# Attention steps in another order, projections over three pairs of PSUM banks, and scores issued two units ahead between transposes

## The chip, the cores and the metric

The kernel runs on one core of one Trainium2 chip. The metric is the device time of one execution, in microseconds (us); less is better. The core's engines are named as in the profile: PE is TensorE's matmul row and PEld its weight loads, DVE is VectorE, ACT is ScalarE, POOL is GpSimd and SP is SyncE, which here only issues DMAs.

## What is computed

Two layers of a streaming encoder, over 1024 prompt tokens and 64 sample tokens, width 1024. Each layer is

```python
xn = rmsnorm(x, norm_pre)
a_x, a_g, b_q, ..., c_v, c_g = split(xn @ w_in)
y_a = rg_lru(causal_conv(a_x)) * silu(a_g)            # width 512
y_b = top-k sparse attention, 4 heads * silu(b_g)     # width 256
y_c = differential attention, 4 heads * silu(c_g)     # width 256: softmax1 - lam * softmax2, normed per head
x = x + rmsnorm(concat(y_a, y_b, y_c) @ w_out, norm_post)
```

The attention is causal by chunks of 64 tokens, so query tile t (128 tokens) reads 128 (t + 1) keys; the sample tile reads 1024 cached keys and its own 64. All is computed in fp32. The kernel returns x of the last layer and each layer's states.

## The kernel before

Each layer has a front (input projection, convolution and recurrence, the indexer's scores, the search for the top-k threshold) and then the attention stage, which alone the change touches. The attention stage takes the nine query tiles in the order 7, sample, 6, 0, 1, 2, 3, 4, 5 (`ORDER`). Each tile has four C units (one head each, with two softmax maps, except in the sample tile, where a C unit has one map of stacked queries) and four B units (two in the sample tile), 70 units in all. `schedule()` (L123) writes out one list, `STEPS`, and every engine walks through the same list and takes what is its own, in order:

- `qk` i, m: TensorE computes the scores of a map into one of two PSUM slots (L1692 to L1702), VectorE takes the negative maximum (L1454), ScalarE the exponential and its row sum (L1141).
- combining unit i (`combine`, L575): VectorE takes the reciprocal of the sum and, for a C unit, mixes the two maps with `scalar_tensor_tensor` (L585 to L597). The transposes of the unit wait for it (L1714). In the kernel before it is tied to the first `qk` of the next unit (L1449).
- `tr` i, g: TensorE transposes up to four blocks of 128 keys into one PSUM bank (L1717); ScalarE (C units) or VectorE (B units) copies them out (L570). All groups and all `ytr` share this one bank, so each waits for the copy of the one before (L1712).
- `pv` i: TensorE multiplies the transposed weights with the values into the output bank (L1736); VectorE scales the result (`divide`, L599: L613 to L627, where a C unit also sums its squares). In the kernel before it is tied to the first `tr` of the next unit (L1463).
- `ytr` n: the finished heads of the n-th tile, once GpSimd has gated them, are transposed (L1746) and copied out by ScalarE (L1157).
- `proj` n, q: 16 steps of the output projection of tile n (8 for the sample tile), L1775 and L1770, into PSUM banks 2 and 3 (`mixb`, L394). Step 0 waits until the rows of the tile before have been taken out of them (`mix_drained`, L1755). `QUOTA` (L90) says how many steps a unit may carry.
- `square` n on ScalarE (L1178, L1172, L1175), 1/sqrt on GpSimd (L937, L939), `rows` n on VectorE (L1481, L1477), the residual added on GpSimd (L946), the store on SP (L735).

A tile is called wide here where it has more than 512 keys (7, sample, 6, 4, 5: two or three groups of transposes) and narrow otherwise (0 to 3: one group). Scores use PSUM banks 0 to 2 and 3 to 5; outside the sample tile the second slot is banks 4 and 5, so that 2 and 3 are free for the projections. In a wide unit i the list is: first map of `qk` i+1, `rows`, second map, `proj`, `tr` i 0, `proj`, `pv` i-1, the other groups of `tr` i, and `ytr` in the third unit of a tile. In a narrow one: first map, one `proj`, `pv` i-1, `rows`, second map, the other `proj` steps, `tr` i. When a projection ends, the next one may start two units later (`hold`, L144). GpSimd prepares the padded queries of the tiles to come at certain `qk` steps (L902 to L908).

## Time and profile before

| | us |
|---|---|
| median of three runs | 1717.11 (1715.88 to 1722.72) |
| the profiled execution | 1713.17 |
| its span, first to last instruction | 1711.4 |
| TensorE busy | 1579.6 (92% of the span) |
| VectorE busy | 1130.6 (66%) |
| ScalarE busy | 626.8 (37%) |
| GpSimd busy | 425.3 (25%) |
| granted TensorE clock, mean | 0.973 |

The first layer's attention stage lies at 463 to 860 us of the span, the second one's at about 1311 to 1711. Rows of a timeline give the start, the duration, the engine, the line, the operation with its tiles, and in brackets the idle time before it with what ended it. A duration of a matmul includes its way through the array, so neighbouring rows overlap; a step's length is best read from start to start.

### The profile page before, as it was taken

The page shows a single profiled execution, that of the slowest core. Times are in us where ns is not written, and L with a number is a line of the kernel's source. Part 1 is how long each engine was busy: PE and PEld are TensorE (multiplying, and loading weights), DVE is VectorE, ACT ScalarE, POOL GpSimd, SP SyncE. Part 2 cuts the span into 40 slices and gives each one's busy share as a digit, 9 for nine tenths or more (in the row PEclk, how much of TensorE's full clock was granted, in tenths as well). Part 3 has the DMA queues.
Part 4 walks back from the last instruction along what each step waited for, and adds up shares of the span by engine and source line. Part 5 has one row for each costly group of instructions (what it writes and reads, how often), then busy time and mean ns, then how long its engine had stood idle before and what let it go on. Part 6 is the DMA issues. An engine that isn't in the chain of part 4 may idle for free. (4 is left out here: it accounts for less than half of the span.)

```text
span 1711.4 us, 21022 instructions
## 1 busy us (share of the span) xinstructions
PE 1579.6 (92%) x7276; PEld 1083.2 (63%) x7298; DVE 1130.6 (66%) x2456; ACT 626.8 (37%) x1227; POOL 425.3 (25%) x540
## 2 busy tenths in 40 slices
PE   6999999999988889999859999999999888899996
PEld 3566566688876755567435665666888667555663
DVE  3478999948963655465134789999589646545550
ACT  2285520228143333333022756202280433333330
POOL 2001621520020344342120016205200213444411
PEclk9999999999998999999979999999999999999999
DMA  5100001321050311110151000013210503111101
GB/s 175 53 25 25 25 25 50 100 76 35 1 185 4 113 38 58 40 38 32 49 187 53 25 25 25 25 50 99 65 47 0 183 6 117 42 52 37 51 24 56
DMA packets 39177, 99.19 MB, mean 58 GB/s; under 512 B 8672, under 2 KB 27616, under 8 KB 34720
## 3 DMA queue, kind: packets, MB, share of 16 engines
q1 hardware_dynamic: 39072, 97.85, 17.3%
q8 instruction: 59, 0.97, 0.2%
q14 instruction: 46, 0.38, 0.1%
HBM read 66.84 MB, written 18.14 MB: 50 GB/s over the span
## 5 line engine op out<-in xcount | busy, mean ns | idle before, releaser
L1551 PE MATMUL ps<-r_xn,r_w 128*128 128x384 f32 (+1 forms) x1728 | 555.3, 473 | 12.3 <-DVE r_xn L1218 7.5
L1551 PEld LDWEIGHTS ps<-r_xn,r_w 128*128 128x128 f32 x1728 | 326.0, 191 | 195.7 <-issue 18.5
L1319 DVE TENSOR_SCALAR_CACHE_REDUCE r_ix<-r_sc,smi 128x768 bf16<-128x768 f32 (+6 forms) x380 | 342.0, 962 | 2.2
L1141 ACT ACTIVATE r_sc<-ps,sm 128x1024 f32<-128x1024 f32 (+8 forms) x204 | 155.7, 764 | 346.4 <-DVE sm L1454 339.2
L1454 DVE TENSOR_REDUCE sm<-ps 128x1 f32<-128x1024 f32 (+8 forms) x204 | 157.2, 784 | 121.8 <-PE ps L1699 52.1
L1627 PE MATMUL ps<-r_w,r_xn 128*128 128x256 f32 x1024 | 223.4, 380 | 0.0
L1627 PEld LDWEIGHTS ps<-r_w,r_xn 128*128 128x128 f32 x1024 | 193.9, 190 | 27.3 <-issue 1.0
L1736 PEld LDWEIGHTS ps<-r_vg,r_w 128*128 128x128 f32 (+1 forms) x1176 | 149.9, 194 | 52.9 <-issue 25.4
L1736 PE MATMUL ps<-r_vg,r_w 128*128 128x64 f32 (+1 forms) x1176 | 151.9, 274 | 6.3 <-DVE r_w L613 3.0
L1717 PE MATMUL ps<-ident,r_sc 128*128 128x128 f32 (+1 forms) x684 | 118.0, 282 | 39.1 <-ACT r_w L570 28.1
L1775 PE MATMUL ps<-r_xn,r_ag 128*128 128x512 f32 x256 | 137.5, 644 | 14.4 <-DVE r_res L1481 11.4
L1717 PEld LDWEIGHTS ps<-ident,r_sc 128*128 128x128 f32 (+1 forms) x684 | 83.7, 148 | 95.4 <-issue 46.8
L1775 PE MATMUL ps<-r_xn,r_vg 128*128 128x512 f32 x256 | 126.8, 604 | 0.1
L1281 DVE SCALAR_TENSOR_TENSOR r_sc<-r_vg,sm,r_sc 128x384 f32<-128x384 f32 (+6 forms) x98 | 97.8, 998 | 28.9 <-ACT r_vg L1056 23.4
L1056 ACT ACTIVATE r_vg<-ps 128x384 f32<-128x384 f32 (+6 forms) x112 | 88.4, 795 | 29.9 <-PE ps L1588 24.3
L570 DVE COPY r_w<-ps 128x512 f32<-128x512 f32 (+3 forms) x104 | 58.7, 565 | 60.3 <-PE ps L1717 59.3
L613 DVE TENSOR_SCALAR r_w<-ps,sm 128x64 f32<-128x64 f32 x128 | 35.7, 279 | 80.0 <-PE ps L1736 80.0
L1696 PE MATMUL ps<-kst_c,qc_hi 128*128 128x512 f32 (+3 forms) x192 | 79.4, 414 | 3.5 <-ACT r_sc L1141 2.0
L570 ACT COPY r_w<-ps 128x512 f32<-128x512 f32 (+3 forms) x112 | 55.0, 491 | 61.9 <-PE ps L1717 61.9
L1775 PEld LDWEIGHTS ps<-r_xn,r_ag 128*128 128x128 f32 x256 | 46.9, 208 | 41.4 <-issue 25.8
L783 POOL COPY sm<-r_ax 128x3 f32<-128x3 f32 x8 | 4.0, 501 | 271.3 <-ACT r_ax L995 271.3
L1588 PE MATMUL ps<-iks,iqs 128*128 128x384 f32 (+3 forms) x160 | 68.7, 500 | 1.5 <-ACT iqs L1038 1.5
(244 smaller groups left out, 2068.5 us busy)
## 6 DMA issues: line engine op xcount, KB each, us to landing
r_w<-w_in SPq DMA_DIRECT2D x28, 1024.0 KB, 4.9
r_xn<-w_out SPq DMA_DIRECT2D x2, 4096.0 KB, 13.5
y<-r_res SPq DMA_DIRECT2D x16, 512.0 KB, 2.9
r_vg<-x SPq DMA_DIRECT2D x8, 512.0 KB, 9.9
r_xn<-ckT SPq DMA_DIRECT2D x2, 2048.0 KB, 8.3
r_xn<-vcache SPq DMA_DIRECT2D x2, 2048.0 KB, 13.8
o_v<-r_vg SPq DMA_DIRECT2D x4, 1024.0 KB, 11.1
r_sc<-x SPq DMA_DIRECT2D x8, 512.0 KB, 4.9
```

The costliest lines, as they stand in the source:

```text
L570: ins = copy(pT[i % 2][:, k0:k1, 0:r], src[:, 0:k1 - k0, 0:r])
L1056: drains_x(nc.scalar.activation(dst, src, ACT.Relu, scale=scale), key)
L1141: ins = nc.scalar.activation(ex[2 * (i % 2) + m][0:r, 0:w], on_slot(s, w, r), ACT.Exp, bias=negm[0:r, c:c + 1], accum_out=den[0:r, c:c + 1])
L1281: ins = vec.scalar_tensor_tensor(sc[t][0:r, 0:w], src, iw[0:r, t, h:h + 1], sc[t][0:r, 0:w], ALU.mult, ALU.add)
L1319: ins = vec.tensor_scalar(unsel[t][0:rows(t), :], sc[t][0:rows(t), :], b, None, op, ALU.add, accum_out=cnt[0:rows(t), c:c + 1])
L1454: vec.tensor_reduce(negm[0:r, c:c + 1], on_slot(s, w, r), X, ALU.max, negate=True)\
L1551: ins = nc.tensor.matmul(on_ring(key, cn), w[:, k, P * s:P * (s + 1)], xnT[:, k, c0:c0 + cn], start=(k == 0), stop=(k == KT - 1))
L1627: ins = nc.tensor.matmul(on_ring(key)[:, BW * (t - t0):BW * (t - t0 + 1)], xnT[:, k, P * t:P * (t + 1)], w[:, k, :], start=(k == 0), stop= ...
L1696: ins = nc.tensor.matmul(out, q, kst[kind][:, h, c0:c0 + cn], start=(n2 == 0), stop=(n2 == 1 and not more))
L1717: ins = nc.tensor.transpose(tbank[0:kn, P * (k - 4 * g):P * (k - 4 * g) + r], ex[2 * (i % 2)][0:r, P * k:P * k + kn], ident[0:r, 0:r])
L1736: ins = nc.tensor.matmul(obank[0:r, 0:vals.shape[1]], pT[i % 2][0:kn, k, 0:r], vals, start=(k == 0), stop=(k == nk - 1))
L1775: ins = nc.tensor.matmul(mixb[:, half, :], yk, wo[:, k, BANK * half:BANK * (half + 1)], start=(k == 0), stop=(k == KT - 1))
```

## The change

Three PSUM places for the projections instead of one, `combine` and `divide` as steps of their own, another order of the list, and the scores of unit i+2 between the transposes of unit i in the sample tile and in the B units of wide tiles.

- `mix_place`: projections of the 2nd and 4th tile in the order go to banks 4 and 5, that of the 8th to banks 0 and 1, the others to banks 2 and 3. For this the second slot of narrow tiles moves to bank 1 (`on_slot`). A projection waits only for the rows of the tile that had the same place before. The scores of the first unit of tile 4 get a wait for the fourth tile's rows and for the map before.
- `qk` is split: `exp` is ScalarE's part and may stand later in the list than `qk`. `comb` and `div` are VectorE's and stand in the list.
- `ytr` moves from behind the transposes of its unit to ahead of them. `rows` comes one unit (wide) or two units (narrow) after its projection's end, in wide tiles ahead of `comb`. Where the place differs, the next projection follows without a pause. The projection of the 8th tile is kept until after the last unit.
- In the sample tile and the B units of wide tiles the order of unit i is: `rows`, `ytr`, one `proj`, `tr` i 0, `qk` i+2 (if units i+1 and i+2 have one map each), `proj`, `tr` i 1, `pv` i-1, `div` i-1, `tr` i 2, `exp` i+2, and then the next unit begins with `comb` i+1. This is so in 14 of the 70 units.

```diff
@@ -89,6 +89,8 @@
 YTR = 2
+NARROW_MIX = (1, 3)
+NARROW_END = 7
 LAST_ROWS = [("tm", "cv", 3), ("tm", "cv", 4)]
+def mix_place(n):
+
+    return 1 if n in NARROW_MIX else 2 if n == NT - 2 else 0
+def same_place(n):
+
+    return [m for m in range(n) if mix_place(m) == mix_place(n)]
@@ -127,49 +139,76 @@
+    def scores(i):
+
+        new = []
+        if begun[0] <= i < len(units):
+            begun[0] = i + 1
+            if i:
+                new.append(("comb", i - 1))
+            for m in range(maps_of(i)):
+                new += [("qk", i, m), ("exp", i, m)]
+        return new
     def take(i, most):
         new = []
         while waiting and most and i >= hold[0]:
-            n, q = waiting.pop(0)
+            n, q = waiting[0]
+            if n >= NT - 2 and i < len(units):
+                break
+            waiting.pop(0)
             new.append(("proj", n, q))
             most -= 1
             if q == proj_steps(ORDER[n]) - 1:
                 new.append(("square", n))
-                finish.append(n)
-                hold[0] = i + 2
+                late = 1 if width(units[min(i, len(units) - 1)][0]) > BANK else 2
+                finish.append((i + late, n))
+                if mix_place(n + 1) == mix_place(n):
+                    hold[0] = i + late + 1
         return new
...
-        pv = [("pv", i - 1)] if i else []
-        steps += nxt[:1]
+        pv = [("pv", i - 1), ("div", i - 1)] if i else []
+        n = NTH[i]
+        ytr = []
+        if i - FIRST[n] == YTR and n:
+            ytr = [("ytr", n - 1)]
+        nxt = scores(i + 1)
+        if not nxt:
+            nxt = [("comb", i)]
         if len(groups) == 1:
-            steps += take(i, 1) + pv + rows_now + nxt[1:] + take(i, quota - 1) + groups
+            steps += nxt[:3] + take(i, 1) + pv + rows_now + nxt[3:] + ytr + take(i, quota - 1) + groups
+        elif t == SAMPLE or (True and kind == "B"):
+
+            steps += nxt
+            steps += rows_now + ytr + take(i, 1) + groups[:1]
+            ahead = []
+            if i + 2 < len(units) and maps_of(i + 1) == maps_of(i + 2) == 1:
+                ahead = [("qk", i + 2, 0), ("exp", i + 2, 0)]
+                begun[0] = i + 3
+            steps += ahead[:1] + take(i, quota - 1) + (groups[1:2] + pv if ahead else pv + groups[1:2])
+            steps += groups[2:] + ahead[1:]
         else:
-            steps += rows_now + nxt[1:] + take(i, 1) + groups[:1] + take(i, quota - 1) + pv + groups[1:]
+            steps += rows_now + nxt + ytr + take(i, 1) + groups[:1] + take(i, quota - 1) + pv + groups[1:]
...
-        steps += new + ([("rows", new[-1][1])] if new[-1][0] == "square" else [])
-    steps.append(("ytr", NT - 1))
+        steps += new + ([("rows", new[-1][1])] if new[-1][0] == "square" and new[-1][1] < NT - 2 else [])
+    steps += [("ytr", NT - 1), ("rows", NT - 2)]
@@ -391,7 +430,8 @@
-        mixb = ps[:, 2 * BANK:4 * BANK].rearrange("p (s b) -> p s b", s=2)
+        banks = ps[:, :].rearrange("p (s b) -> p s b", b=BANK)
+        mixbs = [banks[:, 2:4, :], banks[:, 4:6, :], banks[:, 0:2, :]]
@@ -494,7 +534,7 @@
-                slot = slot[:, BANK:]
+                slot = slot[:, BANK:] if width(ATT[key[1]][0]) > BANK else ps[0:r, BANK:2 * BANK]
@@ -1446,8 +1487,6 @@
-                            if m == 0 and i >= 1:
-                                combine(dve, link, i - 1, first[i - 1])
@@ -1455,18 +1494,16 @@
-                            i, g = s[1], s[2]
-                            if g == 0 and i == len(ATT) - 1:
-                                combine(dve, link, i, first[i])
-                            if ATT[i][1] == "B":
-                                evac_pT(dve, vec.tensor_copy, i, g)
-                            if g == 0 and i >= 1:
-                                divide(dve, i - 1, link)
-                        elif s[0] == "pv" and s[1] == len(ATT) - 1:
+                            if ATT[s[1]][1] == "B":
+                                evac_pT(dve, vec.tensor_copy, s[1], s[2])
+                        elif s[0] == "comb":
+                            combine(dve, link, s[1], first[s[1]])
+                        elif s[0] == "div":
                             divide(dve, s[1], link)
@@ -1669,6 +1706,9 @@
+                            if h == 0 and m == 0 and n == NARROW_END:
+                                pe.wait_ge(mix_drained, NARROW_MIX[-1] + 1)
+                                wait_drained(pe, MAPS[SLOT[s] - 1])
@@ -1750,13 +1790,17 @@
-                                if n:
-                                    pe.wait_ge(mix_drained, n)
-                                else:
-                                    last = FIRST[ORDER.index(SAMPLE) + 1] - 1
-                                    wait_drained(pe, ("qk", last, 0))
-                                    wait_drained(pe, ("qk", last - 1, 0))
+                                if same_place(n):
+                                    pe.wait_ge(mix_drained, same_place(n)[-1] + 1)
+                                if mix_place(n) == 2:
+                                    wait_drained(pe, MAPS[-1])
+                                    wait_drained(pe, MAPS[-2])
+                                if not same_place(n):
+                                    wide = FIRST[ORDER.index(SAMPLE) + (1 if n == 0 else 2)] - 1
+                                    wait_drained(pe, ("qk", wide, 0))
+                                    wait_drained(pe, ("qk", wide - 1, 0))
```

## Rows read from the trace of the kernel before

**Rows 1.** Windows, PE alone: stretch, length, busy (instructions), granted clock, DMA share, GB/s
```profile
499.40:516.50 17.10, 17.10 (x120) 1.00 0.10 30
516.50:555.90 39.40, 32.44 (x179) 0.87 0.00 1
555.90:599.10 43.20, 38.61 (x244) 0.92 0.31 112
599.10:742.00 142.90, 131.44 (x613) 0.95 0.17 50
742.00:773.70 31.70, 29.57 (x172) 1.00 0.04 11
773.70:821.00 47.30, 44.58 (x270) 1.00 0.15 49
821.00:857.00 36.00, 29.62 (x67) 0.90 0.09 31
```
**Rows 2.** Waits of PE, 462 to 860 us: total, times, longest
```profile
PE ps L1775 <- DVE r_res L1481: 5.7, 3, 3.1
...
PE ps L1770 <- DVE r_res L1481: 1.4, 1, 1.4
```
**Rows 3.** Timeline, end of the first layer: start, us, engine, line, operation
```profile
829.71 3.60 PE L1775 MATMUL ps<-r_xn,r_vg 128*128 128x512 f32 x8
...
833.34 1.02 ACT L1178 ACTIVATE r_w<-ps 128x1024 bf16<-128x1024 f32 x1 [19.27 <-PE ps L1775]
...
834.35 0.59 ACT L1157 ACTIVATE r_vg<-ps 128x512 f32<-128x512 f32 x1
...
835.47 1.28 DVE L1481 SCALAR_TENSOR_TENSOR r_res<-ps,sm,r_ix 128x1024 f32<-128x1024 f32 x1 [13.91 <-POOL sm L939]
836.81 6.58 PE L1775 MATMUL ps<-r_xn,r_ag 128*128 128x512 f32 x8 [3.07 <-DVE r_res L1481]
```
**Rows 4.** Timeline of PE, B units of tile 7
```profile
505.64 0.61 PE L1717 MATMUL ps<-ident,r_sc 128*128 128x128 f32 x4
...
507.92 1.90 PE L1736 MATMUL ps<-r_vg,r_w 128*128 128x64 f32 x16
509.65 0.61 PE L1717 MATMUL ps<-ident,r_sc 128*128 128x128 f32 x4
```
**Rows 5.** Timeline of DVE: divide and reciprocal of B units
```profile
625.55 0.28 DVE L613 TENSOR_SCALAR r_w<-ps,sm 128x64 f32<-128x64 f32 x1
625.86 0.16 DVE L585 RECIPROCAL sm<-sm 128x1 f32<-128x1 f32 x1
```
**Rows 6.** Timeline, a C unit of the sample tile
```profile
533.97 0.29 DVE L616 TENSOR_SCALAR r_w<-ps,sm 64x64 f32<-64x64 f32 x1 [1.25 <-PE ps L1736]
...
535.17 0.16 DVE L590 TENSOR_TENSOR sm<-sm 64x1 f32<-64x1 f32 x1
...
535.88 0.42 PE L1717 MATMUL ps<-ident,r_sc 128*64 128x128 f32 x1 [0.68 <-ACT r_w L570]
```
**Rows 7.** Timeline, a C unit of tile 4 (640 keys, wide)
```profile
747.32 1.08 PE L1775 MATMUL ps<-r_xn,r_ag 128*128 128x512 f32 x2
...
749.40 0.58 ACT L570 COPY r_w<-ps 128x512 f32<-128x512 f32 x1
```
**Rows 8.** Timeline, C units of tile 3 (512 keys, narrow)
```profile
707.26 0.68 ACT L1141 ACTIVATE r_sc<-ps,sm 128x512 f32<-128x512 f32 x1
...
708.07 0.60 PE L1717 MATMUL ps<-ident,r_sc 128*128 128x128 f32 x4
708.16 0.16 DVE L592 RECIPROCAL sm<-sm 128x1 f32<-128x1 f32 x1 [0.78 <-ACT r_sc L1141]
...
709.39 0.68 DVE L1454 TENSOR_REDUCE sm<-ps 128x1 f32<-128x512 f32 x1
...
713.17 0.60 PE L1717 MATMUL ps<-ident,r_sc 128*128 128x128 f32 x4
```
**Rows 9.** Timeline of PE, end of the second layer
```profile
1687.26 3.70 PE L1775 MATMUL ps<-r_xn,r_ag 128*128 128x512 f32 x8 [3.07 <-DVE r_res L1481]
```

More of the change, by code:

```diff
@@ L129, in schedule @@
     hold = [FIRST[ORDER.index(SAMPLE) + 1] + FIRST_PROJ]
-    def qk(i):
-        return [("qk", i, m) for m in range(maps_of(i))]
+    begun = [0]
+    def scores(i):
[7 more added lines that the diff above has]
+        return new
     def take(i, most):
@@ L142, in take @@
                 new.append(("square", n))
-                finish.append(n)
-                hold[0] = i + 2
+                late = 1 if width(units[min(i, len(units) - 1)][0]) > BANK else 2
+                finish.append((i + late, n))
+                if mix_place(n + 1) == mix_place(n):
+                    hold[0] = i + late + 1
         return new
-    steps += qk(0) + LAST_ROWS
+    steps += scores(0) + LAST_ROWS
     for i, (t, kind, h) in enumerate(units):
@@ L150, in schedule @@
         groups = [("tr", i, g) for g in range(-(-nk // 4))]
-        nxt = qk(i + 1) if i + 1 < len(units) else []
-        rows_now = [("rows", finish.pop(0))] if finish else []
+        rows_now = [("rows", finish.pop(0)[1])] if finish and finish[0][0] <= i else []
         quota = QUOTA.get(t, 0)
-        pv = [("pv", i - 1)] if i else []
-        steps += nxt[:1]
-        if len(groups) == 1:
-            steps += take(i, 1) + pv + rows_now + nxt[1:] + take(i, quota - 1) + groups
-        else:
-            steps += rows_now + nxt[1:] + take(i, 1) + groups[:1] + take(i, quota - 1) + pv + groups[1:]
-        n = NTH[i]
-        if i - FIRST[n] == YTR and n:
-            steps.append(("ytr", n - 1))
+        pv = [("pv", i - 1), ("div", i - 1)] if i else []
[6 more added lines that the diff above has]
+            nxt = [("comb", i)]
+        if len(groups) == 1:
+            steps += nxt[:3] + take(i, 1) + pv + rows_now + nxt[3:] + ytr + take(i, quota - 1) + groups
[8 more added lines that the diff above has]
+            steps += groups[2:] + ahead[1:]
+        else:
+            steps += rows_now + nxt + ytr + take(i, 1) + groups[:1] + take(i, quota - 1) + pv + groups[1:]
+        if ytr:
             waiting += [(n - 1, q) for q in range(proj_steps(ORDER[n - 1]))]
@@ L165, in schedule @@
     hold[0] = last
-    steps.append(("pv", last - 1))
-    steps += [("rows", n) for n in finish]
+    steps += [("pv", last - 1), ("div", last - 1)]
+    steps += [("rows", n) for _, n in finish]
     while waiting:
@@ L1132, in _ @@
                     for s in STEPS:
-                        if s[0] == "qk":
+                        if s[0] == "exp":
                             i, m = s[1], s[2]
@@ L1140, in _ @@
                                 act.wait_ge(t_filled, last + 1)
-                            ins = nc.scalar.activation(ex[2 * (i % 2) + m][0:r, 0:w], on_slot(s, w, r), ACT.Exp,
+                            ins = nc.scalar.activation(ex[2 * (i % 2) + m][0:r, 0:w], on_slot(("qk", i, m), w, r), ACT.Exp,
                                                        bias=negm[0:r, c:c + 1], accum_out=den[0:r, c:c + 1])
-                            drains(ins, s)
+                            drains(ins, ("qk", i, m))
                             nmap += 1
@@ L1162, in _ @@
                             act.wait_ge(mix_filled, n + 1)
+                            mixb = mixbs[mix_place(n)]
                             if n >= 1:
@@ L1469, in _ @@
                             r = rows(ORDER[n])
+                            mixb = mixbs[mix_place(n)]
                             dve.wait_ge(rso_ready, n + 1)
```

1 line of the change is left out of this document (added).

## The prediction

> **What bounds the kernel now.** I first read the stages of the first layer's attention as a table of TensorE's busy time [rows 1]. TensorE is the bound: from 499 to 857 us it works in most of every stage, and what is lost is idle time between its own instructions (0 of 17.1 us in the four B units of tile 7, 7.0 of 39.4 in the sample tile, 11.5 of 142.9 in the narrow tiles, 2.1 and 2.7 in the two wide tiles behind them) and a clock under 1.00. The second layer runs the same list of steps and loses the same waits. TensorE's work isn't changed by the edit, so the question is only how much idle time the new list leaves. The waits of TensorE say who ends them [rows 2]: 5.7 and 1.4 us a layer go to projections that wait until the rows of the tile before have left the two PSUM banks that all tiles share; 3.07 of them lie at the end of the layer [rows 3], 4.0 inside. That is what the alternating banks remove. Of the rest most is a transpose waiting for the copy of the group before it.
>
> I then wrote out the step list of both kernels and laid the durations of the trace along every place where the lists differ. An estimate below means such a chain.
>
> **Two units ahead in the B units of tile 7.** Now a B unit takes 4.01 us and TensorE is full: its second group of transposes starts at 505.64 and that of the next unit at 509.65 [rows 4]. Nothing is left to hide there. The new list puts the scores of unit i+2 between the two groups, but puts `div` of unit i-1 ahead of `comb` of unit i+1 on VectorE, and TensorE's next step behind `pv` i-1 is the transpose that needs this `comb`. So each such unit gets a round trip: values end, VectorE divides (0.31 us to the reciprocal's start) and takes the reciprocal (0.16) [rows 5], and the signal back costs 0.06 (VectorE's row of 835.47 ends at 836.75, the matmul that waits for it starts at 836.81 [rows 3]; I take 0.1). With the 0.17 us by which the next transposes now overlap the values' row (507.92 + 1.90 against 509.65 [rows 4]) I take 0.8 us for each; 1.0 where the divided unit is a C unit (it also squares) or the next one is the sample tile's (a longer `comb`). Four of them lie in a row here: 3.6 us. Bounds: 0.5 to 1.2 each.
>
> **The sample tile.** Now a C unit waits for the first copy and 0.68 us for the second [rows 6], which with the overlap that is lost makes 1.2 to 1.9 a unit. The new list hides both behind scores and values, but sets the round trip in their place, and it is long: from the divide's start at 533.97 to the end of `comb` at 535.33 are 1.36 us [rows 6]. Against some 6.4 us of such waits in the stage (7.0 idle in all [rows 1]) I get 6.8 with the moved `ytr`: +0.4. The same list for tile 6 and the first B units of tile 4 has a projection step (0.86 us: four of them run from 829.71 to 833.14 [rows 3]) between `pv` and the transpose, which covers the trip: 0.
>
> **`ytr` moved ahead of the transposes.** It shares their bank, so tr i.0 now waits for ScalarE's copy of `ytr` (0.59 us [rows 3]), which stands behind the exponential of the second map. In a wide C unit scores end at 747.3, where the projection starts, and ScalarE's next copy starts at 749.40 [rows 7]; so a transpose behind it could start at 747.3 + 2.1 + 0.6 + 0.1 = 750.1, and TensorE has only the four transposes of `ytr`, some 0.45 us, for these 2.8. The old place of `ytr` waits too, for one copy alone. For tile 6, wider still and with no projection in between: +1.5, between 0 and 3.
>
> **Narrow tiles.** The mix waits of these tiles go (4.0 us), and the projection steps that were held back for them run earlier. The price is that they run out. A projection of tile n can't begin before `ytr` n, and the list has 80 steps for 96 places, so the gaps gather in front of `ytr` 4 and 5, in C units 38, 39 and 46, 47; now they lie mostly in B units, which are cheap. What an uncovered C unit costs: at 708 the unit takes 5.1 us from transpose to transpose (708.07 to 713.17 [rows 8]), of which three projection steps of 0.86 are 2.6, so TensorE has 2.5 us of its own. The loop through the others is: exponential of the second map to the start of `comb` 0.90, `comb` 1.23 up to the next max, two max of 0.68 [rows 8], a divide with its square of about 0.5 (estimated from the 0.31 of the divide above) between them and a signal: 4.1 us. So 1.6 us idle a unit, 1.3 more where `rows` (1.28 us on VectorE [rows 3]) falls in it, and then `ytr` with no projection step behind it, about 3.5. Laid out with the durations of each width this is 6.1 us ahead of `ytr` 4, 7.0 ahead of `ytr` 5 and 1 elsewhere: 14 against 11.5. +2.5. Bounds: if half of it hides, -4; if VectorE also loses time to GpSimd, +5.
>
> **Tiles 4 and 5 (the wide ones at the end).** Nine projection steps that covered them are used up in the narrow tiles, two more are kept for the end. In units 54 to 56 nothing stands between tr.0, `pv` and tr.1: scores end at 747.3, tr.1 can't start before 749.40 + 0.58 + 0.1 = 750.1, and TensorE has the values (ten matmuls, of which 16 take 1.73 us [rows 4]: 1.1) and 0.4 of transposes for these 2.8, so 1.3 idle each. Besides, `rows` stands now ahead of `comb` in VectorE's order, one unit after the projection ends. From the end of a projection, about 833.1: the square starts at 833.34, `rows` on VectorE at 835.47 and ends at 836.75 [rows 3], so 3.6 us; then `comb` 1.5 at these widths, and the next transposes wait for it: 1.4 us at unit 55, 2.8 at unit 65. By chain: tile 4 7.5 us idle against 2.1 (+5.4), tile 5 9.1 against 2.7 (+6.4; in it two bare round trips of 1.0 and 0.8, and `ytr` 7 with one projection step behind it, 2.0). Bounds of the two together: +5 (a half) to +14.
>
> **End of the layer.** Projection 8 no longer waits for `rows` 7: now 3.07 us idle [rows 3]. It still needs `ytr` 8, whose copy (834.35) ends at 834.94, so it starts at 835.1 instead of 836.8: -1.7. In the first layer the clock fell in this gap (eight matmuls took 6.58 us [rows 3], in the second layer 3.70 [rows 9]); if the shorter gap prevents that, -3 once.
>
> **The other moved steps.** GpSimd pads queries at the first scores of a tile; of the scores moved ahead none passes a gating step of GpSimd. SP's stores and loads of `rows` go one or two units later, and POOL's add of `rows`; the next tile's `rows` is at least two units on. The waits on `same_place` come after rows that are long done. The new wait of the first scores of unit 54 has nothing late before it. Cost 0, and 1 us for each if that cover were gone.
>
> **Sum.** 3.6 + 0.4 + 1.5 + 2.5 + 5.4 + 6.4 - 1.7 = 18.1 us a layer, 36 in two, less 3 for the clock: +33. The profiled execution took 1713.2 us (span 1711.4); that makes 1746. It lies 3.9 under the median of the three runs, 1717.1, so I forecast 1750.
>
> **Rivals.** (a) Faster: the uncovered places cost no more than they do in the B units now, since VectorE and ScalarE then have no rows to do in between. Then all the idle time of the narrow tiles that such waits make, 8 of the 11.5 us, and 1.7 at the end are won, 3.6 + 0.4 go to the round trips, and a clock fall of 3 us a layer goes with the gaps: about -8.5 a layer, 1700. For it: the waits it removes are measured ones [rows 2]. Against it: [rows 7, 8], which show the chains longer than the work left beside them. It decides if `comb` doesn't stand in the way, and the loop of 4.1 us says it does. The Trainium skill (Perfetto Trace Analysis, Matmuls) says that independent matmul groups should rotate through different PSUM banks so that the evacuation of one overlaps the next; by that rule alone the change wins, as in (a). (b) No change: the terms are half of what I take and more clock is won than lost, 1717. (c) Slower still: the new gaps of 2 to 3.6 us, four or five a layer against two or three now, each bring the clock to its lower level of 1.2 GHz, as the gap before 836.81 did [rows 3]. The stage from 821 to 857 had 0.90 granted [rows 1], 3.6 us lost. Three more such falls a layer: +20 us, 1770. Against it: in the second layer the same gap of 3.07 us brought no fall [rows 9]. The Trainium skill (TensorE: Matmul & The Clock Gate, Why this matters for your kernels) asks for no long idle gaps between bursts of matmuls; by that rule this rival is the likeliest. That the change doesn't do what it says is excluded: the list has the early scores in 14 of 70 units.
>
> **Chances.** Forecast, slower by 10 to 45 us: 0.60. (c): 0.14. (b): 0.12. (a): 0.14. A measurement of this kernel can tell some 0.5% (8.6 us) from no change. Faster 0.14, same 0.12, slower 0.74. The forecast's own range is 1730 to 1762; the range given, 1712 to 1768, takes in (b) and half of (c), and leaves out (a) and the worst of (c), some 0.2.
>
> **What would show it.** Right: in the profile after, TensorE's transposes wait for VectorE's `comb` (now L585, L590, L597); tile 7's B units take 4.8 us; gaps of over 2 us at the transposes of units 40, 48, 56, 64, 65; waits on `rows` gone; TensorE idle near 57 us a layer against 40. Wrong: the B units still at 4.0, or wide tiles at the end no longer than now by more than the moved projections account for. The forecast fails if VectorE runs `div` late without TensorE waiting, or if the copies are ready sooner in shorter units than the chains say.

## The result, and the profile after

| | before | after |
|---|---|---|
| median of four runs each | 1716.5 us | 1758.8 us (1756.9 to 1760.8) |
| ratio | | 1.025 (95% interval 1.022 to 1.029) |
| span of the profiled execution | 1711.4 us | 1755.1 us |
| granted TensorE clock, mean | 0.973 | 0.956 |

The changed kernel is slower by 42 us. In the changed kernel the transposes are L1757 (they were L1717), the values L1776 (L1736), the scores L1736 to L1742 (L1696 to L1702), the projections L1819 (L1775), `comb` L625 to L637 (L585 to L597), `div` L653 (L613), the copies of transposes L610 (L570), the copy of `ytr` L1197 (L1157), `rows` L1518 (L1481).

The pages' groups of instructions, the two that matter (busy time and mean ns | idle time before them and what ended most of it), before and then after:

```profile
L1717 PE MATMUL ps<-ident,r_sc 128*128 128x128 f32 (+1 forms) x684 | 118.0, 282 | 39.1 <-ACT r_w L570 28.1
...
L1775 PE MATMUL ps<-r_xn,r_ag 128*128 128x512 f32 x256 | 137.5, 644 | 14.4 <-DVE r_res L1481 11.4
```
```profile
L1757 PE MATMUL ps<-ident,r_sc 128*128 128x128 f32 (+1 forms) x684 | 122.7, 290 | 80.2 <-ACT r_vg L1197 24.5
...
L1819 PE MATMUL ps<-r_xn,r_ag 128*128 128x512 f32 x256 | 133.5, 631 | 3.3 <-ACT r_vg L1197 2.7
```

The projections hardly wait any more: 3.3 us over both layers instead of 14.4. The transposes wait 80 us instead of 39. TensorE's waits in the first layer, the answer to [rows 2] (engine, line, what ended the wait: total us, times, longest):

```profile
PE ps L1757 <- ACT r_vg L1197: 12.8, 6, 3.0
PE ps L1757 <- ACT r_w L610: 9.8, 8, 2.7
PE ps L1757 <- DVE r_sc L637: 6.0, 3, 3.9
PE ps L1757 <- DVE sm L625: 5.5, 7, 1.1
```

None is on `rows` any more, where [rows 2] had 5.7 and 1.4 (and a line that it doesn't show, for the rows of the sample tile, 1.3). In their place stand the copy of the moved `ytr`, the operation of `comb` that mixes two maps (L637) and the reciprocal of the B units (L625).

To lay the two kernels side by side I cut both layers at the first matmul of the values of units 0, 7, 13, 21, 53, 61 and 69, because the list has these once a unit in the same order. The windows of the first layer of the changed kernel (stretch, length, busy time and instructions of TensorE, granted clock, share of DMA, GB/s):

```profile
484.20:523.50 39.30, 33.87 (x225) 1.00 0.45 162
523.50:565.60 42.10, 34.97 (x205) 0.88 0.03 7
565.60:607.50 41.90, 37.64 (x237) 0.92 0.30 114
607.50:751.40 143.90, 131.34 (x601) 0.96 0.16 48
751.40:799.20 47.80, 42.09 (x210) 0.79 0.11 34
799.20:840.00 40.80, 31.18 (x193) 0.92 0.08 27
```

And of the kernel before, the last three:

```profile
604.10:744.20 140.10, 128.47 (x585) 0.95 0.17 50
744.20:782.60 38.40, 36.44 (x213) 1.00 0.14 42
782.60:819.70 37.10, 34.38 (x210) 1.00 0.06 17
```

With the same windows in the second layer, "idle" being length less busy time, and the projection steps that the list has in each stage:

| stage (values of units) | length before, layers 1 / 2 | after | idle before | after | projection steps before, after |
|---|---|---|---|---|---|
| tile 7 and sample (0 to 13) | 79.3 / 78.2 | 81.4 / 79.8 | 10.8 / 10.9 | 12.5 / 13.8 | 0, 0 |
| tile 6 (13 to 21) | 40.6 / 38.5 | 41.9 / 40.4 | 3.0 / 3.8 | 4.3 / 4.3 | 6, 6 |
| narrow tiles (21 to 53) | 140.1 / 136.7 | 143.9 / 142.5 | 11.6 / 11.5 | 12.6 / 8.9 | 74, 82 |
| tile 4 (53 to 61) | 38.4 / 38.4 | 47.8 / 48.0 | 2.0 / 2.0 | 5.7 / 6.7 | 14, 12 |
| tile 5 (61 to 69) | 37.1 / 37.0 | 40.8 / 40.7 | 2.7 / 2.7 | 9.6 / 9.6 | 12, 4 |
| sum | 335.5 / 328.8 | 355.8 / 351.4 | 30.2 / 30.9 | 44.7 / 43.3 | 106, 104 |

A step takes 0.86 us of TensorE, so lengths of a stage compare only with its steps beside them: tile 5 grew by 3.7 us although eight steps, 6.9 us of work, had left it.

The attention grew by 20.3 and 22.6 us. The stretch between the two layers' windows (521.6 us before, 522.2 after) and the end behind the second one (41.3 and 41.5) stayed, with the two moved steps (1.7 us) now in each of them. 27 us of the 43 are idle time (14.5 + 12.4). The rest is matmuls that take longer: busy time went from 305.3 to 311.1 and from 297.9 to 308.1 us, with two projection steps fewer inside (1.7 us a layer), so 19 us for the same work. The granted clock shows why. The 10 us windows around units 54 to 56, and the two waits that lie in them:

```profile
740.00:750.00 10.00, 10.00 (x55) 1.00 0.11 27
750.00:760.00 10.00, 5.76 (x28) 0.71 0.03 8
760.00:770.00 10.00, 8.53 (x38) 0.50 0.31 106
770.00:780.00 10.00, 10.00 (x46) 0.77 0.08 20
780.00:790.00 10.00, 10.00 (x58) 1.00 0.05 12
```
```profile
754.74 0.48 PE L1757 MATMUL ps<-ident,r_sc 128*128 128x128 f32 x1 [2.35 <-ACT r_w L610]
...
759.83 1.09 PE L1757 MATMUL ps<-ident,r_sc 128*128 128x128 f32 x4 [1.89 <-DVE r_sc L637]
```

TensorE stands still for 2.35 us before 754.74 and 1.89 us before 759.83, and then runs ten microseconds at 0.50, the lower level of 1.2 GHz: four transposes take 1.09 us there, and 0.63 us at 1.00. Before the change this tile had 1.00 throughout [rows 1].

### The profile page after: what moved, and what is told of

Same layout as the page of the kernel before. It is cut to its first block and busy times, and to the rows that moved or that the text cites. A ratio compares the mean times of both kernels' runs of the same rounds, so it can differ in the third digit from the quotient of the medians.

```text
span 1755.1 us, 21012 instructions
## 1 busy us (share of the span) xinstructions
PE 1599.2 (91%) x7276; PEld 1102.4 (63%) x7298; DVE 1136.3 (65%) x2456; ACT 626.1 (36%) x1227; POOL 422.8 (24%) x540
## 5 line engine op out<-in xcount | busy, mean ns | idle before, releaser
L1588 PE MATMUL ps<-r_xn,r_w 128*128 128x384 f32 (+1 forms) x1728 | 559.0, 475 | 12.5 <-issue 7.9
L1757 PE MATMUL ps<-ident,r_sc 128*128 128x128 f32 (+1 forms) x684 | 122.7, 290 | 80.2 <-ACT r_vg L1197 24.5
L1776 PEld LDWEIGHTS ps<-r_vg,r_w 128*128 128x128 f32 (+1 forms) x1176 | 158.3, 204 | 50.1 <-issue 22.3
L1757 PEld LDWEIGHTS ps<-ident,r_sc 128*128 128x128 f32 (+1 forms) x684 | 84.3, 150 | 139.3 <-issue 64.1
L1776 PE MATMUL ps<-r_vg,r_w 128*128 128x64 f32 (+1 forms) x1176 | 160.4, 284 | 8.4 <-ACT r_w L610 7.2
L1819 PE MATMUL ps<-r_xn,r_ag 128*128 128x512 f32 x256 | 133.5, 631 | 3.3 <-ACT r_vg L1197 2.7
L1819 PE MATMUL ps<-r_xn,r_vg 128*128 128x512 f32 x256 | 128.5, 612 | 0.0
L653 DVE TENSOR_SCALAR r_w<-ps,sm 128x64 f32<-128x64 f32 x128 | 36.1, 282 | 134.8 <-PE ps L1776 134.8
L610 DVE COPY r_w<-ps 128x512 f32<-128x512 f32 (+3 forms) x104 | 58.9, 566 | 70.9 <-PE ps L1757 70.1
L610 ACT COPY r_w<-ps 128x512 f32<-128x512 f32 (+3 forms) x112 | 55.2, 492 | 86.1 <-PE ps L1757 86.1
L1736 PE MATMUL ps<-kst_c,qc_hi 128*128 128x512 f32 (+3 forms) x192 | 81.6, 425 | 4.6 <-ACT r_sc L1181 3.0
L1736 PE MATMUL ps<-kst_c,qc_lo 128*128 128x512 f32 (+3 forms) x192 | 69.9, 376 | 0.0
```

Source lines behind the costliest of these rows:

```text
L610: ins = copy(pT[i % 2][:, k0:k1, 0:r], src[:, 0:k1 - k0, 0:r])
L1588: ins = nc.tensor.matmul(on_ring(key, cn), w[:, k, P * s:P * (s + 1)], xnT[:, k, c0:c0 + cn], start=(k == 0), stop=(k == KT - 1))
L1736: ins = nc.tensor.matmul(out, q, kst[kind][:, h, c0:c0 + cn], start=(n2 == 0), stop=(n2 == 1 and not more))
L1757: ins = nc.tensor.transpose(tbank[0:kn, P * (k - 4 * g):P * (k - 4 * g) + r], ex[2 * (i % 2)][0:r, P * k:P * k + kn], ident[0:r, 0:r])
L1776: ins = nc.tensor.matmul(obank[0:r, 0:vals.shape[1]], pT[i % 2][0:kn, k, 0:r], vals, start=(k == 0), stop=(k == nk - 1))
L1819: ins = nc.tensor.matmul(mixb[:, half, :], yk, wo[:, k, BANK * half:BANK * (half + 1)], start=(k == 0), stop=(k == KT - 1))
```

## The experiments

Each starts from the changed kernel, unless it says otherwise. "Attention" is the time from the values of unit 0 to those of unit 69 in the two layers; the changed kernel has 355.8 and 351.4, the kernel before 335.5 and 328.8.

| kernel | median us | against after | attention, us | projection steps inside |
|---|---|---|---|---|
| before | 1714.8 to 1716.5 | | 335.5 / 328.8 | 106 |
| after | 1758.8 | | 355.8 / 351.4 | 104 |
| e1 no early scores in B units | 1752.6 | -6.2 | 352.6 / 349.8 | 104 |
| e2 `comb` before `div` | 1738.4 | -20.4 | 346.2 / 343.6 | 104 |
| e3 `ytr` back | 1745.3 | -13.5 | 349.3 / 346.5 | 104 |
| e4 `rows` behind `comb` | 1742.5 | -16.3 | 349.0 / 347.4 | 104 |
| e6b even pace | 1721.8 | -37.0 | 337.5 / 331.5 | 102 |
| h1 no addition on GpSimd | 1744.0 | -14.8 | 353.1 / 351.1 | 104 |
| o1 old order, two PSUM places | 1735.6 | -23.2 | 346.0 / 347.0 | 112 |
| o2 o1 with the end mended | 1725.8 | -33.0 | 346.4 / 346.1 | 112 |
| o3 o2 with even pace | 1697.2 | -61.6 | 325.3 / 325.6 | 104 |
| g1 all four amended | 1680.2 | -78.6 | 316.6 / 316.1 | 102 |
| g2 g1 without early scores | 1692.7 | -66.1 | 322.6 / 322.8 | 102 |
| g3 g1, early in the sample tile only | 1682.2 | -76.6 | 316.8 / 315.9 | 102 |

The kernel before was timed beside each group of these; its medians were 1714.8 to 1716.5 us, single executions 1706.4 to 1727.0. The part ahead of the attention is the same code in all of them, and its length still differs: the values of unit 0 begin between 482.8 and 487.4 us. So a difference of two or three microseconds between two kernels isn't read below. Where the steps inside differ, 0.86 us for each belongs to them: o1 has six more than the kernel before, 5.2 us a layer.

**The round trip behind the early scores.**

```diff
-        elif t == SAMPLE or (True and kind == "B"):
+        elif t == SAMPLE or (False and kind == "B"):
```

> The changed kernel, but the B units of wide tiles issue no scores two units ahead (the sample tile still does). Theory of the round trip (divide, then `comb`, then the signal back, 0.7 to 0.9 us a unit where no projection step lies between): the four B units of tile 7 go back from 21.0 to about 17.1 us and units 66 and 67 lose their waits of 0.8 and 0.7, so -5.5 us a layer, -11 in all, about 1748. Rival, that the early scores cost nothing and the time went to the clock alone: tile 7 stays at 21 us and the whole is within 3 us of 1759. Rival, that the early scores also hide something now (the copies in the wide B units): tile 7 falls to 18 or 19 only, -4 to -6 in all.

TensorE's waits in tile 7's B units went, and those of 0.81 and 0.67 us behind units 66 and 67 too. A B unit of tile 7 is back at 4.0 us (505.10 to 509.12), so the third explanation, that the early scores hide something there, is out. But a new wait of 0.82 us, for a copy on ScalarE, stands in the first unit of the sample tile. Idle time fell by 3.5 and 1.9 us in the two layers, the median by 6.2: right direction, about half of the -11 expected. In the first layer the sample tile then ran at 0.84 instead of 0.88, which took part of it back. (The ratio to the kernel before, 1.020, is known to 0.006, some 10 us, so the size stays rough.) The next kernel keeps the early scores and changes only VectorE's order (`rden` holds the reciprocals, now in four places by i % 4):

```diff
                 begun[0] = i + 3
+                combed.add(i + 1)
+                pv = pv[:1] + [("comb", i + 1)] + pv[1:]
...
-        rden = sm[:, 160:164]
+        rden = sm[:, 228:236]
...
```

> The changed kernel, with `comb` of unit i+1 ahead of `div` of unit i-1 on VectorE in the 14 units with early scores, and the reciprocals in four places instead of two so that neither overwrites the other. Theory of the round trip: what TensorE waits for is only the order on VectorE, so the waits on `comb` in tile 7 (0.67 to 0.86) and in the sample tile (0.98 to 1.30) go: -3 in tile 7, -3 to -4 in the sample tile, -1 in tile 5, so -7 to -8 us a layer, about 1744. Rival, that the exponential is what is late (it stands behind the last group's copy on ScalarE): then `comb` can't run earlier, and less than 5 us of the whole go. Rival, that the early scores themselves cost: 0.

-20.4 us, somewhat more than expected. The timeline of the changed kernel and then of this one, the same B unit of tile 7 (start, us, engine, line, operation, in brackets the idle time before and what ended it):

```profile
509.15 0.29 DVE L653 TENSOR_SCALAR r_w<-ps,sm 128x64 f32<-128x64 f32 x1 [0.35 <-PE ps L1776]
...
509.47 0.16 DVE L625 RECIPROCAL sm<-sm 128x1 f32<-128x1 f32 x1
509.78 0.63 PE L1757 MATMUL ps<-ident,r_sc 128*128 128x128 f32 x4 [0.67 <-DVE sm L625]
```
```profile
505.19 0.15 DVE L628 RECIPROCAL sm<-sm 128x1 f32<-128x1 f32 x1
505.72 0.61 PE L1760 MATMUL ps<-ident,r_sc 128*128 128x128 f32 x4
505.92 0.28 DVE L656 TENSOR_SCALAR r_w<-ps,sm 128x64 f32<-128x64 f32 x1 [0.57 <-PE ps L1779]
```

In the first the reciprocal stands behind the divide, and the transposes start 0.31 us after the reciprocal's start. In the second it is done 0.4 us before the transposes, which wait for nothing. Units 0 to 13 took 72.2 and 72.0 us (after: 81.4 and 79.8; before: 79.3 and 78.2). So with `comb` ahead of `div` these units are 7.1 and 6.2 us shorter than before the change; 2.8 and 3.1 of that are idle time, the rest is the clock of the sample tile (0.89 and 0.92 before, 1.00 here). Of the 9.2 and 7.8 us that this one swap won against the changed kernel, 4.5 and 6.0 are idle time; the clock of the sample tile went from 0.88 and 0.96 to 1.00.

**`ytr` behind the transposes again.**

```diff
-            steps += nxt[:3] + take(i, 1) + pv + rows_now + nxt[3:] + ytr + take(i, quota - 1) + groups
+            steps += nxt[:3] + take(i, 1) + pv + rows_now + nxt[3:] + take(i, quota - 1) + groups
...
-            steps += rows_now + nxt + ytr + take(i, 1) + groups[:1] + take(i, quota - 1) + pv + groups[1:]
+            steps += rows_now + nxt + take(i, 1) + groups[:1] + take(i, quota - 1) + pv + groups[1:]
+        steps += ytr
```

> The changed kernel with `ytr` again behind the transposes of its unit. Theory that the moved `ytr` costs what its copy stands behind on ScalarE (waits of 2.25, 2.91, 2.96, 1.47 and 2.28 us a layer behind that copy, against some 0.5 us each in the old place): -7 to -9 us a layer, -14 to -18 in all, about 1743, and a lower-clock stretch or two less. Rival, that these units are short of covering work whatever the place of `ytr` (no projection step left in them): the waits only change their name to the copies of the transposes, and less than 5 us of the whole go.

-13.5 us: just short of the theory's lower edge. But it holds only in the wide tiles (tile 6 -3.6 and -2.1 us, tile 4 -3.5 and -3.6, tile 5 -1.9 and -1.8), and there only in part by the waits: idle time of the whole attention fell by 1.2 us in the first layer and 5.1 in the second, of 6.5 and 4.9 us of length. In the first layer tile 4 even had 0.6 us more idle time and was shorter because its clock was 0.92 instead of 0.79. In the narrow tiles the length stayed (144.4 and 143.6 against 143.9 and 142.5), and the rival is right there. The wait of unit 40, in the changed kernel (with the `rows` ahead of it on VectorE) and in this one:

```profile
680.44 1.28 DVE L1518 SCALAR_TENSOR_TENSOR r_res<-ps,sm,r_ix 128x1024 f32<-128x1024 f32 x1
...
683.43 0.90 PE L1757 MATMUL ps<-ident,r_sc 128*128 128x128 f32 x3 [2.91 <-ACT r_vg L1197]
```
```profile
681.32 0.90 PE L1787 MATMUL ps<-ident,r_w 128*128 128x128 f32 x3 [2.90 <-ACT r_w L611]
```

The same 2.9 us, once in the transposes behind the copy of `ytr`, once in `ytr` behind the copy of the transposes. Both copies stand behind the exponential of the second map on ScalarE, and TensorE has no projection step. In the changed kernel that exponential starts at 682.22, after the maximum that VectorE takes at 681.63, directly behind `rows`: as the prediction had it, `rows` (1.28 us) is in this chain. No run moves `rows` alone in the narrow tiles.

**`rows` behind `comb`.**

```diff
-            steps += rows_now + nxt + ytr + take(i, 1) + groups[:1] + take(i, quota - 1) + pv + groups[1:]
+            steps += nxt[:3] + rows_now + nxt[3:] + ytr + take(i, 1) + groups[:1] + take(i, quota - 1) + pv + groups[1:]
```

> The changed kernel with `rows` behind `comb` and the first maximum of its unit in the C units of wide tiles. Theory that `rows` holds up `comb` in units 55 and 65 (waits of 1.89 and 3.87 us): both go but for some 0.6 us that the missing projection steps leave, so -4 to -5 us a layer, -9 in all, about 1750. Rival, that the units are only short of projection steps: the wait moves to the exponential or to the second maximum that `rows` now delays, and the whole stays within 3 us of 1759.

-16.3 us, where -9 was expected. The wait of 1.89 us ahead of unit 55 went and that of 3.87 us ahead of unit 65 became 1.05. Idle time in tiles 4 and 5 fell by 6.1 us in the two layers, but their length by 14.1: tile 4 ran at 0.85 and 0.92 instead of 0.79 and 0.82, tile 5 at 0.95 instead of 0.92. A microsecond of idle time there went with more than two of length. The attention makes up 10.8 of the 16.3 us; the rest lies in parts whose code is the same.

Unit 65 in the changed kernel shows a second thing:

```profile
816.83 1.28 DVE L1518 SCALAR_TENSOR_TENSOR r_res<-ps,sm,r_ix 128x1024 f32<-128x1024 f32 x1
...
818.19 2.34 POOL L986 TENSOR_TENSOR r_res<-r_res,r_sc 128x1024 f32<-128x1024 f32 x1 [1.73 <-DVE r_res L1518]
...
818.59 2.76 DVE L637 SCALAR_TENSOR_TENSOR r_sc<-r_sc,sm 128x768 f32<-128x768 f32 x1
...
821.49 0.63 PE L1757 MATMUL ps<-ident,r_sc 128*128 128x128 f32 x4 [3.87 <-DVE r_sc L637]
```

`comb` takes 2.76 us while GpSimd adds the residual; where nothing runs beside it, this operation takes 1.02. At unit 55 it is 2.63 against 0.89. So `rows` ahead of `comb` costs twice: its own 1.28 us, and 1.7 us because its addition is released just as `comb` starts. This kernel leaves out nearly all of the residual addition, so its outputs are not the layer's:

```diff
-                            nc.gpsimd.tensor_tensor(res[0:r, :], res[0:r, :], xres[0:r, :], ALU.add)\
+                            nc.gpsimd.tensor_tensor(res[0:r, 0:8], res[0:r, 0:8], xres[0:r, 0:8], ALU.add)\
```

> The changed kernel with GpSimd's addition of the residual (it follows each `rows`) cut to 8 of the 1024 columns, so it leaves out nearly all of that sum; all waits and the order of the list stay. In the changed kernel `comb`'s last operation took 2.63 and 2.76 us at units 55 and 65 while that addition ran (2.34 us), and 1.02 us at 768 columns where none ran. Theory that VectorE's operation with two SBUF inputs stands still while GpSimd adds: both fall to 0.9 and 1.0 us, the waits ahead of units 55 and 65 from 1.89 and 3.87 us to about 0.2 and 2.1, so some 3.4 us a layer and with the clock they bring down 10 to 14 us in all, about 1747. Rival, that these two operations are long for another reason (the order behind `rows`, a slow reading of PSUM before): they stay over 2 us, and the whole within 3 us of 1759.

Unit 65 with it:

```profile
813.53 1.28 DVE L1518 SCALAR_TENSOR_TENSOR r_res<-ps,sm,r_ix 128x1024 f32<-128x1024 f32 x1
...
814.89 0.20 POOL L986 TENSOR_TENSOR r_res<-r_res,r_sc 128x8 f32<-128x8 f32 x1 [2.25 <-DVE r_res L1518]
...
815.28 1.02 DVE L637 SCALAR_TENSOR_TENSOR r_sc<-r_sc,sm 128x768 f32<-128x768 f32 x1
```

The operation is back at 1.02 us (0.88 at unit 55) and the wait ahead of unit 65 at 1.03 us: the stall is GpSimd's. The time also fell by about what was expected, 14.8 us, and yet not for the reason given. The attention became only 2.7 and 0.3 us shorter. Tile 5 lost 3.0 us of idle time and 0.6 us of length, because its clock fell from 0.92 to 0.83; ahead of unit 55 1.55 of the 1.89 us of waiting stayed. Most of the gain lies outside: 6.1 us between the two attentions and 2.3 behind the second one, where the last addition of a layer (2.3 us) stands on the path to its end. In 220 us of the stretch between them, from 40 us behind the attention on, the granted clock was 0.97 and 0.94 in the changed kernel; why, these runs don't show.

**The PSUM places alone, and the pace of the projections.** These three keep the order of the kernel before (`comb`, `div` and `exp` are steps of their own, at their old places). Against that kernel, and beside the banks and waits of the change:

```diff
+def mix_place(n):
+    return 1 if n in NARROW_MIX else 0
...
-                hold[0] = i + 2
+                if mix_place(n + 1) == mix_place(n):
+                    hold[0] = i + 2
```

> The order of the list as before the change (`comb`, `div`, `ytr`, `rows` in their old places, no early scores), with only the second PSUM place for the projections of the 2nd and the 4th tile and no pause where the place differs; the last two tiles share one place as before. Theory that the projection steps run out: the 4.0 us a layer of waits on `rows` inside go, but units 38, 39, 46, 47 and 54 to 55 have no projection step, 1.3 to 1.6 us idle each, so 0 to +4 us a layer, 1716 to 1724. Rival, the bank rule alone: -4 us a layer and some clock, about 1706.

1735.6 us, 1.012 of the kernel before (1.008 to 1.015): +20 us from an edit that removes waits and lets the next projection follow at once. Both expectations were too good. Idle time rose by 4.3 and 3.7 us in the two layers, as the theory had it at its worst; another 10 us are longer matmuls for the same work, which neither counted. The waits on `rows` inside went, and the projection steps ran out. Unit 40's neighbourhood in this kernel:

```profile
675.51 0.88 PE L1769 MATMUL ps<-r_vg,r_w 128*128 128x64 f32 x6 [0.82 <-ACT r_w L603]
...
678.92 0.88 PE L1769 MATMUL ps<-r_vg,r_w 128*128 128x64 f32 x6 [1.29 <-ACT r_w L603]
...
681.30 0.88 PE L1750 MATMUL ps<-ident,r_sc 128*128 128x128 f32 x3 [1.02 <-DVE r_sc L630]
683.31 0.90 PE L1779 MATMUL ps<-ident,r_w 128*128 128x128 f32 x3 [1.14 <-ACT r_w L603]
```

There is no projection between them, and each of these waits for VectorE or ScalarE. Idle time in the narrow tiles is 13.8 and 12.8 us (11.6 and 11.5 before) at a clock of 0.93 and 0.94, against 0.95 and 0.98.

The second kernel gives the last tile's projection banks 0 and 1 and puts `ytr` 8 among the last steps of projection 7:

```diff
-    return 1 if n in NARROW_MIX else 0
+    return 1 if n in NARROW_MIX else 2 if n == NT - 1 else 0
...
+        if n_end(new):
+            new = new[:-5] + [("ytr", NT - 1)] + new[-5:]
...
```

> The kernel of the run before (old order, two places) with the projection of the last tile in banks 0 and 1 and `ytr` 8 between the last steps of projection 7, so that projection 8 waits for nothing. The gap of 3.07 us ahead of projection 8 goes in both layers and the slow stretch behind it in the first one, against the run before: -6 to -9. Rival, that the time comes back as a clock fall elsewhere: -3 or less.

-9.8 us, slightly more than expected. The gap of 3.06 us ahead of projection 8 is gone; from 834.62 on TensorE has no idle time up to the layer's last step. The third changes one number for three of the four narrow tiles:

```diff
-QUOTA = {0: 3, 1: 3, 2: 3, 3: 3, 4: 2, 5: 2, 6: 1}
+QUOTA = {0: 3, 1: 2, 2: 2, 3: 2, 4: 2, 5: 2, 6: 1}
```

> The kernel of the run before with two projection steps a unit instead of three in tiles 1 to 3, so that every unit up to the last has one. Theory that a projection step is worth what it covers: idle time of TensorE in the narrow tiles and tile 4 falls by 6 to 8 us a layer against the run before, and the whole lies under the kernel before the change: 1695 to 1703. Rival, that the copies and `comb` are waited for at any pace: within 4 us of the run before.

-28.5 us against o2, and 0.989 of the kernel before (0.986 to 0.993). Tiles 4 and 5, first in o1, then here:

```profile
753.00:795.20 42.20, 38.95 (x212) 0.88 0.13 38
795.20:832.60 37.40, 34.59 (x211) 1.00 0.09 29
```
```profile
736.80:775.40 38.60, 36.34 (x215) 1.00 0.11 31
775.40:812.70 37.30, 35.87 (x215) 1.00 0.03 13
```

Two more projection steps in each, and tile 4 is still 3.6 us shorter. The same three numbers in the changed kernel; since projection 6 then ends after the last unit, where that list had no `rows` for it, this kernel has a `rows` behind each projection that ends there:

> The changed kernel with the even pace of projection steps (two a unit in tiles 1 to 3) and nothing else; projection 6 now ends behind the last unit, and `rows` 6 follows it. Theory that most of the loss in the narrow tiles and in tiles 4 and 5 is missing cover (the same pace took 28 us from the old order): the waits of 2.9 at units 40 and 48, of 2.35 and 1.89 at 54 and 55, of 2.3 and 3.9 at 64 and 65 shrink to 1 or less each, 9 to 11 us of idle time and two clock falls less a layer, 1725 to 1735. Rival, that the moved `ytr` and `rows` cost the same at any pace: not under 1750.

-37.0 us, more than expected: most of the loss of the change goes with these three numbers. In the attention 10.2 and 10.3 us of it are idle time, 6.4 and 7.9 shorter matmuls for the same work, 1.7 two steps that lie behind it. The narrow tiles took 123.6 and 122.0 us (143.9 and 142.5 after, with 14 steps more, 12 us), all at clock 1.00.

**All of it together.** g1 has e2, e3, e4, e6b and the end of o2; g2 and g3 take the early scores out again, in all 14 units and in the B units.

> The changed kernel with all four amended: `comb` before `div` in the units with early scores, `ytr` behind the transposes, `rows` behind `comb`, the even pace, and `ytr` 8 among the last steps of projection 7. Theory that every loss found is a place in the list and none lies in the early scores or the third PSUM place themselves: the waits that are left are those of the C units of tiles 7 and 6 and of the sample tile's second copy, and the early scores save 3 us a layer in the sample tile, so it lies some 10 us under the old order at even pace (1697): 1682 to 1692. Rival, that the early scores cost what they save once `comb` is right: 1693 to 1700. Rival, that TensorE in the full B units only moves the wait to the copies: over 1700.

> The kernel of the run before without any early scores (14 units back to the plain order of wide units). By the theory the B units stay full either way (4.0 us each), and only the sample tile's waits of 0.68 and 0.61 to 0.97 a unit come back: 5 to 8 us slower than with them, 1688 to 1698. By the rival the two are within 3 us of each other. Against the old order at even pace (1697) it lacks the 1.7 us ahead of projection 7 in each layer: 3 to 5 us less.

> The kernel with all four amended, with early scores in the sample tile alone (not in the B units of tiles 7, 6, 4 and 5). If the B units have nothing to hide, it equals the one with all within 3 us. If a full B unit with early scores still has a wait, it is 2 to 5 us faster than that one; if they hide copies in tiles 4 and 5, as much slower.

g1 is at 1680.2 us, 0.981 of the kernel before (0.978 to 0.984). Its windows, at the same cuts as above:

```profile
484.30:520.30 36.00, 33.39 (x225) 1.00 0.49 175
520.30:557.80 37.50, 32.39 (x207) 0.95 0.03 8
557.80:597.40 39.60, 36.13 (x240) 0.96 0.32 120
597.40:721.70 124.30, 116.18 (x574) 1.00 0.17 51
721.70:759.60 37.90, 36.48 (x216) 1.00 0.10 30
759.60:800.90 41.30, 37.55 (x216) 0.96 0.08 26
```

The narrow tiles and tile 4 run at 1.00, and most of what is left of idle time in tile 5 is 2.64 us at unit 62, the one unit of that tile between two projections that share a place. The four single edits took 9.6, 6.5, 6.8 and 18.3 us from the first layer's attention and 7.8, 4.9, 4.0 and 19.9 from the second one's, 41.2 and 36.6 in sum; together they took 39.2 and 35.3, so inside the attention they hardly overlap. The medians add up less well: 87.2 us for the four and 9.8 for the end as o2 has it, against 78.6 together. Without the early scores it is 12.5 us slower, more than the 5 to 8 expected; units 0 to 13 are 5.1 and 5.9 us longer. Having them in the B units too makes no difference that can be told (2.0 us).

## Why the prediction was right, and where it was not

The forecast was 1750, slower, with 1730 to 1762 of its own; it came to 1758.8. The direction and the named mechanisms stand. The sum came near for a partly wrong reason: inside the attention it had 13 us too much idle time in the two layers and left out 19 us of longer matmuls. That the two nearly cancel is luck. Per layer:

| step, idle time in us | predicted | measured, layers 1 / 2 |
|---|---|---|
| tile 7 and sample (3.6 + 0.4) | +4.0 | +1.7 / +2.9 |
| tile 6, `ytr` | +1.5 | +1.3 / +0.5 |
| narrow tiles | +2.5 | +1.0 / -2.6 |
| tile 4 | +5.4 | +3.7 / +4.7 |
| tile 5 | +6.4 | +6.9 / +6.9 |
| sum of idle time inside | +19.8 | +14.5 / +12.4 |
| longer matmuls for the same work | 0 | +7.5 / +11.9 |

- **Round trip.** Right in mechanism and nearly in size: waits of 0.81, 0.67, 0.67 and 0.86 us, 3.0 instead of 3.6, a unit of 4.85 us (504.93 to 509.78) against 4.01 [rows 4], and e2 removes them by VectorE's order alone. The sample tile was a little better than the even trade that I had laid out (+0.4): without these waits idle time of units 0 to 13 fell by 1.3 and 0.3 us.
- **`ytr` ahead of the transposes.** Right in the wide tiles (2.25, 1.47 and 2.28 us). In the narrow ones the wait belongs to the missing projection steps, as e3 shows; the prediction had put it there.
- **Narrow tiles.** In the first layer waits of 2.91 and 2.96 us stood behind `ytr` 4 and 5, where 3.5 were forecast (2.89 and 1.79 in the second), but the units before them lost less: the step of 1.6 us for every uncovered C unit was too high. Units 38, 39, 46 and 47 waited 0.82, 0.97, 1.35 and 0.73 us, nearer to the half that the bounds allowed.
- **Tiles 4 and 5.** The idle time was nearly right, and for unit 65 (3.87 us, 2.8 predicted) the term was short by GpSimd: `comb` was taken at 1.5 us and took 2.76. The prediction had named that collision only for the narrow tiles, as a bound.
- **The clock.** This is the step that failed. The sum credited 3 us for the gap at the end, and kept clock falls in the rival "slower still", against which it set the gap of 3.07 us without a fall [rows 9]. The gap at the end did shrink (1.35 us, and the eight matmuls behind it took 3.67 us instead of 6.58 [rows 3]), though the stretch between the attentions is no shorter for it. But the new gaps of 2 to 4 us in tiles 4 and 5 did bring the clock down: 1.00 before, 0.79 and 0.82 in tile 4 after, 0.92 in tile 5. The trace of the kernel before already had such a fall, which the prediction didn't use: in its first layer projection 4 waited 2.18 us for `rows`, and the clock was at 0.50 behind it (stretch, length, busy time, granted clock as above):

```profile
690.00:694.00 4.00, 3.59 (x26) 1.00 0.00 0
694.00:696.00 2.00, 0.08 (x2) 0.97 0.00 0
696.00:700.00 4.00, 3.74 (x10) 0.50 0.16 57
```

  Behind the same wait in the second layer (2.19 us) the first two matmuls still ran at full speed (1.12 us instead of 2.07), and the four us from 1548 on had 0.65. So the gap at the end of the second layer, without a fall, was the exception that the prediction took for the case. That rival had the right mechanism and about the right price (20 us; measured 19), and it belonged in the sum, beside less idle time.
- **The signs.** The waits on `comb`, the longer B units and the end of the waits on `rows` came as named. Of the gaps over 2 us, those at units 40, 48, 64 and 65 did; unit 56 waited 1.47 us, and unit 54 2.35, which was forecast at 1.3. TensorE's idle time over the whole span went from 131.8 to 155.9 us, 12 a layer where the signs had 17.
- **The rival "faster"** was that uncovered places cost little and the removed waits are won. o1 comes nearest to that rival as a kernel, and it lost 20 us. The Trainium skill (Perfetto Trace Analysis, Matmuls) says that independent matmul groups should rotate through PSUM banks so that the next group overlaps the evacuation of the one before; by that rule alone o1 had to gain. The trace differs: a projection that waited for its bank was also one that was saved for a unit that had nothing else. With an even pace and the end mended the same banks are part of a kernel 19 us faster than before (o3); what they alone are worth at that pace was not run, nor the even pace in the kernel before with its one place, so how much of the 19 us the banks give is open.

What stays open: how the 19 us of clock divide among the single gaps, since a fall follows some gaps of 2 to 3 us and not others ([rows 3] against [rows 9]); and why the clock between the attentions was higher in h1, where it gained 6 us.

## What to carry to other kernels

Work that can run at any time, such as these projection steps, is the cover of everything else: when a wait in it is removed, check first that it isn't used up early, and spread it so that no unit is without a step. On an in-order engine, put the operation that the bottleneck waits for next ahead of the one that is merely due (`comb` before `div`, `rows` behind `comb`); here two such swaps were worth 20 and 16 us. And price a new gap on TensorE with the clock: in tiles 4 and 5 of e4 6.1 us of idle time less went with 14.1 us less of length, and in h1 3.0 us less of it with next to nothing.

## What the runs showed of the hardware

- **VectorE is held up by GpSimd.** With two SBUF inputs VectorE's operation on 128x768 took 2.76 us while GpSimd's addition of 2.34 us ran, and 1.02 with that addition cut to 0.20 us. It ended 0.82 us after the addition did. A maximum that reads PSUM was not slowed in such an overlap (0.95 us for 768 columns in g1, 0.96 without). The Trainium skill (GPSIMD Engine Reference, Key points) says that GpSimd shares its SBUF interfaces with VectorE and contends with its instructions that have two SBUF inputs. The trace agrees: the operation took 1.74 us more, and 1.94 us of GpSimd's instruction were left when it started.
- **A gap removed can leave the length nearly as it was.** In h1 tile 5 had 3.0 us less idle time and was 0.6 us shorter, at 0.83 granted instead of 0.92.
- **The same code differs in its matmuls' time.** The part ahead of the attention, unchanged in all kernels, ended between 482.8 and 487.4 us. At these two ends (e4 and o3) TensorE was idle for 24.7 and 25.0 us and busy for 458.1 and 462.4.
